# Attention of the first chunk between the q, k and v projections, with the bias table as three tensors, in a hybrid encoder block

## The chip, the cores and the metric

One Trainium2 chip, 8 cores. Each core computes one of the eight batch elements (2048 tokens of 1024 channels) with the same program and all the weights; the cores exchange nothing. The metric is the device time of the slowest core in microseconds (us). The time before the change is a median of three runs.

## The reference

The block computes, for each batch element:

```
x   = LayerNorm_in(x)
u   = x @ W_in              # q 512 | k 128 | v 128 | conv-GLU 1024 | branch gates 2048
y_a = windowed_gqa(q, k, v, rel_bias, sink) @ W_attn_out
y_c = silu(LayerNorm(depthwise_conv31(a * sigmoid(g)))) @ W_conv_out
mix = (sigmoid(g_a) * y_a + sigmoid(g_c) * y_c) @ W_out
h   = LayerNorm1(alpha * x + mix)
out = LayerNorm2(alpha * h + (silu(h @ W_gate) * (h @ W_up)) @ W_down)
```

Attention has 8 query heads in 2 groups that share a key and a value head of 64 channels. A block of 128 queries sees its own block of keys and those on either side, with a relative-position bias by head (masked outside a distance of 128) and a sink logit in the denominator. So 16 query blocks see three key blocks each, the first and the last see two.

## The kernel before

**How the work is tiled.** Tokens go in four chunks (tc) of 512, each of four tiles of 128. `ln_in` (line 531) loads a tile of x, normalises it on VectorE and transposes it into x0T. `glu_block` (560) makes the convolution's input: two projections of 512 tokens, a tanh into `sig` on ScalarE (L566) and a product into `glu` on VectorE (L568). The q, k and v projections are the loop in lines 603 to 627 (L556 with `wqk`, L621 for v), each evicted by ScalarE into qT, kT and vones. The convolution goes through DRAM: glu is stored in four pieces, reloaded transposed as `poly` (634 to 640), and multiplied by tap matrices that VectorE builds (L650) in four groups `conv_mm` (L667, its bias added on VectorE in L671). Its LayerNorm follows: 16 statistics (L481, L484), 16 normalisations (L692), and 16 times four transposes (L701) with a SiLU on ScalarE (L705) into `ycin`.

**Attention** goes in 16 units n, one query block each. `att_front` (717) does, for each of its two or three key blocks, the score products of both groups (L729, one pair on the two halves of the array's rows) into two banks, the scaling and bias on VectorE (L736, one for each bank) and the exp on ScalarE (L742) into one of twelve probability tiles pT. `att_back` (747) does, for each group, the value products (L762), the division on VectorE (L767, L769, L770: add the sink, reciprocal, multiply), and after the second group a transpose (L781) and a copy back into qT (L785). `gate_block` (804) does one eighth of the gated merge of a chunk: two gate projections (L556 with `wga`) with a tanh into `gab` (L813), the products Ya (L822, from attention, needs all four units of the chunk) and Yc (L831, from the convolution), two VectorE steps (L837, L840) and a sum on GpSimd (L843). There are eight gab tiles, so four gate blocks can be open at a time. Then come `mix_tile` (L863) and the feed-forward part (L902, L926).

**What sets the order.** Nothing is ordered by hand. Each operation is added with an engine, an estimated cost and a priority (`sc.prio`, lower is more urgent), and the planner `arrange` (141) simulates the five engines and builds one fixed order for each. On each engine it takes, of the operations that can start at once, the one with the lowest priority value, and otherwise the one that can start first; a switch of ScalarE's table between exp and SiLU is charged with 2.6 us, and a DMA with 2.0 us and then its turn in a single serial stream of 0.19 MB per us. PSUM banks are given out by class (`tr=2, proj=3, sc=4, o=2, y=2, mix=2, gu=6, dn=4, cv=2`). The priorities that matter here: front stage 100 to 135, poly 126, bias loads 140, tap tiles and convolution 155 to 160, its LayerNorm 165, q, k and v of chunk tc at 300 + tc, attention units of chunk c at 400 + 10 c and a little more for each unit, gate blocks of chunk tc at 408 + 10 tc, x0 rows 460.

**What waits for what.** A wait is made for each read and write of the same tensor, and also for bytes that two tensors share: `register` (82) notes the overlaps, and an operation on a tensor waits for all operations, added earlier, on every tensor that overlaps it, whatever part they touch. The byte map is lines 349 to 438. `biast` (399) lies over `lnin` (the two rows of the input LayerNorm, 389) and `sig` (390); the probability tiles pTa and obf (404, 405) lie over the glu weights `wgl` (381); `wao` and `wco` lie over the last wgl and all wqk. SyncE issues the plain loads and stores, GpSimd those that cast to bf16 (the weights).

Of the kernel before, what the change touches and what calls it, by code (L numbers as in the profile page):

```python
# [6 lines left out]
F32 = mybir.dt.float32  # L7
BF16 = mybir.dt.bfloat16
AF = mybir.ActivationFunctionType
ALU = mybir.AluOpType  # L10
# [275 lines left out]
def build():  # L286
    nc = bass.Bass("TRN2", target_bir_lowering=False)

    def din(name, shape):
# [6 lines left out]
    bias_d = din("biasT", [3, 128, 1024])  # L296
# [14 lines left out]
    sc = Sched(dict(tr=2, proj=3, sc=4, o=2, y=2, mix=2, gu=6, dn=4, cv=2),  # L311
               ("xl", "slot", "glu_d", "h_d", "x0_d", "out_d", "gu"))

    def sb(off, shape, dt, name):
        h = nc.alloc_sbuf_tensor_at(name, shape, dt, offset=off)
        nbytes = int(np.prod(shape[1:])) * (4 if dt == F32 else 2)
        assert off >= SBUF_BASE and off + nbytes <= SBUF_TOP, (name, off, nbytes)
        sc.register(name, off, nbytes)
        return h, off + ((nbytes + 31) // 32) * 32

    def sbn(off, n, shape, dt, name):
        hs = []
        for i in range(n):
            h, off = sb(off, shape, dt, "%s%d" % (name, i))
            hs.append(h)
        return hs, off


    o = SBUF_BASE
    ident, o = sb(o, [128, 128], BF16, "ident")  # L330
    ident32, o = sb(o, [128, 128], F32, "ident32")
    small, o = sb(o, [128, C_SMALL], F32, "small")
    hbias, o = sb(o, [128, 16], F32, "hbias")
    esink, o = sb(o, [128, 8], F32, "esink")
    negh, o = sb(o, [128, 8], F32, "negh")
    NST = 8
    stt, o = sbn(o, NST, [128, 12], F32, "st")
    mvX, o = sb(o, [128, 32], F32, "mvX")
    rsX, o = sb(o, [128, 16], F32, "rsX")
    mvC, o = sb(o, [128, 32], F32, "mvC")  # L340
# [9 lines left out]
    YR = R0 + 4 * 8192  # L350
# [15 lines left out]
    def bank(b):  # L366
        return ps[:, b.i * 512:(b.i + 1) * 512]
# [10 lines left out]
    for f in range(8):  # L378
        for w in range(2):
            wga[f + 8 * w] = sb(WG + 2048 * (2 * f + w), [128, 1024], BF16, "wga%d" % (f + 8 * w))[0]  # L380
    wgl, o = sbn(WD_, 8, [128, 1024], BF16, "wgl")
    wqk, o = sbn(o, 6, [128, 1024], BF16, "wqk")
    qT, _ = sb(ER, [128, 4 * S], BF16, "qT")
    kT, _ = sb(KR, [128, S], BF16, "kT")
    vones, _ = sb(KR + 8192, [128, 16 * 130], BF16, "vones")
# [1 line left out]
    lnrow, o = sb(GR, [128, 2 * D], F32, "lnrow")  # L387
    onesr, _ = sb(o, [128, 128], F32, "onesr")
    lnin, o = sb(LS, [128, 2 * D], F32, "lnin")
    sig, _ = sbn(o, 2, [128, 512], F32, "sig")  # L390
    taps, o = sb(TP, [128, 64 * 3 * 16], BF16, "taps")
    cbias, o = sb(o, [128, 512], F32, "cbias")

# [2 lines left out]
    yall, _ = sb(YR, [128, 16 * 512], F32, "yall")  # L396
    tw = [sb(WG + 20480, [128, 16 * 3 * 128], BF16, "tw0")[0], sb(GR, [128, 16 * 3 * 128], BF16, "tw1")[0]]

    biast, _ = sb(LS, [128, 3 * 1024], F32, "biast")
    wao, o = sb(WD_ + 12288, [128, 4 * 1024], BF16, "wao")  # L400
    wco, o = sb(o, [128, 4 * 1024], BF16, "wco")
    assert o <= ER
# [44 lines left out]
    ycv = ycin[:, :].rearrange("p (c r i) -> p c r i", c=4, r=16)  # L447
    qTv = qT[:, :].rearrange("p (h s) -> p h s", h=4)
    vv = vones[:, :].rearrange("p (t g c) -> p t g c", t=16, g=2)
    biasv = biast[:, :].rearrange("p (j c) -> p j c", j=3)  # L450
    woutv = wout[:, :].rearrange("p (k c) -> p k c", k=8)
    waov = wao[:, :].rearrange("p (k c) -> p k c", k=4)
    wcov = wco[:, :].rearrange("p (k c) -> p k c", k=4)
# [14 lines left out]
    def load(kb, dst_ap, src_ap, writes, reads=()):  # L468
        sc.dma("sp", kb, lambda e: e.dma_start(out=dst_ap, in_=src_ap), reads=reads, writes=writes)
# [241 lines left out]

    sc.prio = 140
    for j in range(3):
        load(512, biasv[:, j, :], bias_d[j], [("biast", j)])
    pctr = [0]

    def att_front(n):
        pts = [[], []]
        for j in range(3):
            kb = n + j - 1  # L720
            if not 0 <= kb < 16:
                continue
            Bs = (Bank("sc"), Bank("sc"))

            def f_sc(e, kb=kb, Bs=Bs):
                ins = None
                for g in range(2):
                    r0 = 64 * g
                    ins = e.matmul(bank(Bs[g]).rearrange("p (i q) -> p i q", i=4),  # L729
                                   kT[r0:r0 + 64, kb * 128:(kb + 1) * 128],  # L730
                                   qTv[r0:r0 + 64, :, n * 128:(n + 1) * 128], start=True, stop=True)
                return ins
            sc.add("pe", 0.3, f_sc, reads=[("kT", kb // 4)] + [("qT", i, n) for i in range(4)], writes=list(Bs))
            for g in range(2):
                B = Bs[g]
                sc.add("dve", C_DVE, lambda e, B=B, g=g, j=j: e.scalar_tensor_tensor(  # L736
                    bank(B), bank(B), 0.125, biasv[:, j, g * 512:(g + 1) * 512], ALU.mult, ALU.add),
                    reads=[B, ("biast", j)], writes=[B])
                pi = pctr[0] % NP
                pctr[0] += 1  # L740
                pt = pTb[pi]
                sc.add("act", C_ACT, lambda e, B=B, pt=pt: e.activation(pt[:, :], bank(B), AF.Exp),  # L742
                       reads=[B], writes=[pTn[pi]], table="exp")
                pts[g].append((pi, pt, kb))
        return pts
# [44 lines left out]

    def att_units(us):
        for n in us:
            sc.prio = 400 + (n // 4) * 10 + (n % 4) * 0.2
            for k in range(n, min(n + 2, 16)):
                if k not in fr and k // 4 == n // 4:
                    fr[k] = att_front(k)
            pts = fr.pop(n)
            for g in range(2):
                att_back(n, g, pts[g])
# [310 lines left out]
```

How the kernel before makes its waits and increments, by code:

```python
    def run(self, ename, eng):  # L260
        seen = {}
        def wait(pairs):
            waits = {}
            for sem, val in pairs:
                key = id(sem)
                if key not in waits or waits[key][1] < val:
                    waits[key] = (sem, val)
            for key, (sem, val) in waits.items():
                if seen.get(key, 0) < val:
                    eng.wait_ge(sem, val)
                    seen[key] = val
        for op in self.order[ename]:
            pairs = [d.token for d in op.deps]
            if op.extra is not None:
                pairs.append(op.extra)
            wait(pairs)
            ins = op.fn(eng)
            if op.dma:
                ins.then_inc(op.token[0], 16)
            elif op.sig:
                ins.then_inc(op.token[0], 1)
        wait([o.token for o in self.all if o.dma])
```

## Time and profile before

| | before |
|---|---|
| median of three runs | 916.88 us (915.97 to 917.78) |
| profiled execution, its own time | 915.82 us |
| its span, slowest of 8 cores | 914.3 us (others from 911.4) |
| TensorE busy | 858.4 us, 94% of the span |
| VectorE busy | 504.8 us, 55% |
| ScalarE busy | 244.6 us, 27% |
| GpSimd busy | 198.3 us, 22% |
| DMA moved | 110.62 MB, 121 GB/s in the mean |

How to read it. The profile is one execution, on its slowest core. PE is TensorE's matmul, PEld its weight load (beside PE), DVE VectorE, ACT ScalarE, POOL GpSimd, SP SyncE; a "q" behind a name is the engine's own queue of instructions or DMA issues. L736 is line 736 of the kernel. In a row of instructions "out<-in" names the tensors without buffer numbers, x is the count, and the arrow in brackets says what ended the idle time ahead of it. PEclk is the granted clock of TensorE as a share of its full 2.4 GHz. Times in the trace are in us from the start of the span.

### The profile page before, as it was taken

The page shows a single profiled execution, that of the slowest core. Times are in us where ns is not written, and L with a number is a line of the kernel's source. Part 1 is how long each engine was busy: PE and PEld are TensorE (multiplying, and loading weights), DVE is VectorE, ACT ScalarE, POOL GpSimd, SP SyncE. Part 2 cuts the span into 40 slices and gives each one's busy share as a digit, 9 for nine tenths or more (in the row PEclk, how much of TensorE's full clock was granted, in tenths as well). Part 3 has the DMA queues.
Part 4 walks back from the last instruction along what each step waited for, and adds up shares of the span by engine and source line. Part 5 has one row for each costly group of instructions (what it writes and reads, how often), then busy time and mean ns, then how long its engine had stood idle before and what let it go on. Part 6 is the DMA issues. An engine that isn't in the chain of part 4 may idle for free.

```text
span 914.3 us, 13966 instructions; the slowest of 8 cores (911.4 to 914.3 us)
## 1 busy us (share of the span) xinstructions
PE 858.4 (94%) x4638; PEld 412.8 (45%) x4724; DVE 504.8 (55%) x793; ACT 244.6 (27%) x373; POOL 198.3 (22%) x291
## 2 busy tenths in 40 slices
PE   4899999679999999999999999999999999999994
PEld 1445565534444444444444444444444444444441
DVE  5798348777988967777783212136552121223654
ACT  2233324562635444424332111100001111110000
POOL 4234002214031220523233231112111111100111
PEclk9999999779999999999999999999999999999997
DMA  9876588173342331748779998522345554500321
GB/s 200 197 161 108 124 181 133 55 139 116 117 150 82 116 116 49 182 139 228 172 202 237 167 165 129 83 53 110 116 124 85 84 77 70 82 11 33 107 92 46
DMA packets 47928, 110.62 MB, mean 121 GB/s; under 512 B 12913, under 2 KB 13041, under 8 KB 47473
## 3 DMA queue, kind: packets, MB, share of 16 engines
q0 software_dynamic: 21600, 41.72, 30.3%
q1 hardware_dynamic: 26258, 68.00, 22.5%
q8 instruction: 40, 0.66, 0.3%
q14 instruction: 30, 0.25, 0.1%
HBM read 124.15 MB, written 27.26 MB: 166 GB/s over the span
## 4 chain that ended last, share of the span: by engine, by line
PE 84%; DVE 5%; DMA 4%; issue 4%; ACT 1%; POOL 1%; SPq 0%; DVEq 0%; ACTq 0%; POOLq 0%
PE ps L902 32%; PE ps L556 19%; PE ps L926 17%; PE ps L863 4%; PE ps L831 3%; PE ps L822 2%; DMA h_rows<-xr 2%; PE ps L667 1%; PE ps L729 1%; DMA xr<-x_rows 1%; PE ps L506 1%; DVE st L481 1%; PE ps L701 1%; PE ps L762 1%; DVE ps L736 1%
## 5 line engine op out<-in xcount | busy, mean ns | idle before, releaser
L910 DVE TENSOR_TENSOR hid<-ps,sgb 128x512 bf16<-128x512 f32 x88 | 60.9, 692 | 214.4 <-PE ps L902 211.4
L902 PE MATMUL ps<-hT,wEa 128*128 128x512 bf16 x688 | 153.5, 379 | 1.7 <-DMA xr<-x_rows 0.9
L902 PE MATMUL ps<-hT,wEb 128*128 128x512 bf16 x689 | 153.6, 379 | 0.8
L926 PE MATMUL ps<-wdn,hid 128*128 128x512 bf16 x690 | 151.5, 379 | 0.7
L908 ACT ACTIVATE sgb<-ps 128x512 f32<-128x512 f32 x88 | 52.6, 598 | 313.4 <-PE ps L902 312.6
L556 PE MATMUL ps<-x0T,wga 128*128 128x512 bf16 x492 | 115.9, 379 | 2.3 <-ACT pTb L742 0.7
L926 PEld LDWEIGHTS ps<-wdn,hid 128*128 128x128 bf16 x704 | 68.9, 98 | 83.0
L902 PEld LDWEIGHTS ps<-hT,wEa 128*128 128x128 bf16 x704 | 68.6, 98 | 83.3 <-issue 1.3
L902 PEld LDWEIGHTS ps<-hT,wEb 128*128 128x128 bf16 x704 | 68.7, 98 | 81.9
L843 POOL TENSOR_TENSOR mT<-gab,gab 128x512 bf16<-128x512 f32 x32 | 48.0, 1512 | 131.0 <-DVE gab L837 55.6
L556 PEld LDWEIGHTS ps<-x0T,wga 128*128 128x128 bf16 x512 | 48.7, 98 | 59.8 <-issue 4.5
L813 ACT ACTIVATE gab<-ps,hbias 128x512 f32<-128x512 f32 x64 | 43.8, 688 | 87.9 <-PE ps L556 85.6
L736 DVE SCALAR_TENSOR_TENSOR ps<-ps,biast 128x512 f32<-128x512 f32 x92 | 59.0, 692 | 7.7 <-PE ps L729 7.7
L556 PE MATMUL ps<-x0T,wgl 128*128 128x512 bf16 x251 | 58.2, 391 | 3.0 <-ACT x0T L510 2.5
L863 PE MATMUL ps<-wout,mT 128*128 128x512 bf16 x251 | 57.4, 379 | 0.5 <-DVE rden L769 0.3
L931 DVE SCALAR_TENSOR_TENSOR hr<-hr,ps 128x512 f32<-128x512 f32 x32 | 21.9, 685 | 61.0 <-PE ps L926 61.0
L742 ACT ACTIVATE pTa<-ps 128x512 bf16<-128x512 f32 x71 | 40.8, 599 | 24.7 <-DVE ps L736 23.8
L556 PEld LDWEIGHTS ps<-x0T,wgl 128*128 128x128 bf16 x256 | 25.6, 100 | 34.7 <-issue 6.5
L487 POOL TENSOR_SCALAR rsZ<-mvZ 128x1 f32<-128x1 f32 x16 | 4.7, 291 | 156.2 <-DVE mvZ L484 156.2
L863 PEld LDWEIGHTS ps<-wout,mT 128*128 128x128 bf16 x256 | 24.8, 98 | 29.3 <-issue 0.5
L831 PE MATMUL ps<-ycin,wco 128*128 128x512 bf16 x128 | 33.9, 392 | 4.1 <-ACT ycin L705 2.3
L556 PE MATMUL ps<-x0T,wqk 128*128 128x512 bf16 x152 | 35.3, 379 | 0.4
(96 smaller groups left out, 901.0 us busy)
## 6 DMA issues: line engine op xcount, KB each, us to landing
xa<-x SPq DMA_DIRECT2D x16, 512.0 KB, 6.3
xb<-x SPq DMA_DIRECT2D x16, 512.0 KB, 3.8
x_rows<-xb SPq DMA_DIRECT2D x16, 512.0 KB, 2.8
xr<-x_rows SPq DMA_DIRECT2D x16, 512.0 KB, 5.4
h_rows<-xr SPq DMA_DIRECT2D x16, 512.0 KB, 5.4
hr<-h_rows SPq DMA_DIRECT2D x16, 512.0 KB, 3.3
out<-hr SPq DMA_DIRECT2D x16, 512.0 KB, 2.6
wEa<-wg POOLq DMA_DIRECT2D x22, 256.0 KB, 4.3
```

What stands on the lines that cost most here:

```text
L556: ins = e.matmul(bank(B), w[:, kc, :], x0Tv[tc][:, kc, :], start=(kc == 0), stop=(kc == 7))
L736: sc.add("dve", C_DVE, lambda e, B=B, g=g, j=j: e.scalar_tensor_tensor(bank(B), bank(B), 0.125, biasv[:, j, g * 512:(g + 1) * 512], ALU.mu ...
L742: sc.add("act", C_ACT, lambda e, B=B, pt=pt: e.activation(pt[:, :], bank(B), AF.Exp), reads=[B], writes=[pTn[pi]], table="exp")
L813: sc.add("act", 0.69, lambda e, ga=ga, B=B, w=w: e.activation(ga[:, :], bank(B), AF.Tanh, bias=hbias[:, 8 * w + f:8 * w + f + 1], scale=0. ...
L831: ins = e.matmul(bank(Yc), wcov[:, c, f * 128:(f + 1) * 128], ycv[:, c, :, 32 * tc:32 * tc + 32], start=(c == 0), stop=(c == 3))
L843: sc.add("pool", 1.27, lambda e: e.tensor_tensor(mTv[tc][:, f, :], ga[:, :], gc[:, :], ALU.add), reads=[gan, gcn], writes=["mT%d" % tc] + ...
L863: ins = e.matmul(bank(B), mTv[tc][:, kc, i * 128:(i + 1) * 128], woutv[:, kc, half * 512:(half + 1) * 512], start=(kc == 0), stop=(kc == 7))
L902: ins = e.matmul(bank(B), w[:, kc, :], hTv[tc][:, kc, :], start=(kc == 0), stop=(kc == 7))
L908: sc.add("act", C_ACT, lambda e, G=G, sg=sg: e.activation(sg[:, :], bank(G), AF.Silu), reads=[G], writes=[sn], table="silu")
L910: sc.add("dve", C_DVE, lambda e, U=U, sg=sg, c2=c2: e.tensor_tensor(hid[ffc][:, c2 * 512:(c2 + 1) * 512], bank(U), sg[:, :], ALU.mult), re ...
L926: ins = e.matmul(bank(B), hid[k][:, c0:c0 + 128], wdn[k][:, half * 512:(half + 1) * 512], start=(k == 0), stop=(k == NFF - 1))
L931: sc.add("dve", C_DVE, lambda e, half=half, B=B: e.scalar_tensor_tensor(xs[:, half * 512:(half + 1) * 512], xs[:, half * 512:(half + 1) * ...
```

## The change

The glu weights are laid out in the order c, c+4 instead of 0 to 7 in a row. `sig` moves from behind `lnin` to the start of the yall region (YR). The bias table becomes three tensors, one for each key block, in the same bytes as before. Their loads have priority 122 instead of 140. Units 0 to 3 have priority 301.1 and up instead of 400 and up, all others keep theirs. The paired score products are as they were, and nothing else differs.

```diff
--- before.py
+++ after.py
@@ -378,8 +378,11 @@
     for f in range(8):
         for w in range(2):
             wga[f + 8 * w] = sb(WG + 2048 * (2 * f + w), [128, 1024], BF16, "wga%d" % (f + 8 * w))[0]
-    wgl, o = sbn(WD_, 8, [128, 1024], BF16, "wgl")
-    wqk, o = sbn(o, 6, [128, 1024], BF16, "wqk")
+    wgl = [None] * 8
+    for c in range(4):
+        for w in range(2):
+            wgl[c + 4 * w] = sb(WD_ + 2048 * (2 * c + w), [128, 1024], BF16, "wgl%d" % (c + 4 * w))[0]
+    wqk, o = sbn(WD_ + 16384, 6, [128, 1024], BF16, "wqk")
     qT, _ = sb(ER, [128, 4 * S], BF16, "qT")
     kT, _ = sb(KR, [128, S], BF16, "kT")
     vones, _ = sb(KR + 8192, [128, 16 * 130], BF16, "vones")
@@ -387,7 +390,7 @@
     lnrow, o = sb(GR, [128, 2 * D], F32, "lnrow")
     onesr, _ = sb(o, [128, 128], F32, "onesr")
     lnin, o = sb(LS, [128, 2 * D], F32, "lnin")
-    sig, _ = sbn(o, 2, [128, 512], F32, "sig")
+    sig, _ = sbn(YR, 2, [128, 512], F32, "sig")
     taps, o = sb(TP, [128, 64 * 3 * 16], BF16, "taps")
     cbias, o = sb(o, [128, 512], F32, "cbias")
 
@@ -396,7 +399,7 @@
     yall, _ = sb(YR, [128, 16 * 512], F32, "yall")
     tw = [sb(WG + 20480, [128, 16 * 3 * 128], BF16, "tw0")[0], sb(GR, [128, 16 * 3 * 128], BF16, "tw1")[0]]
 
-    biast, _ = sb(LS, [128, 3 * 1024], F32, "biast")
+    biast, _ = sbn(LS, 3, [128, 1024], F32, "biast")
     wao, o = sb(WD_ + 12288, [128, 4 * 1024], BF16, "wao")
     wco, o = sb(o, [128, 4 * 1024], BF16, "wco")
     assert o <= ER
@@ -447,7 +450,6 @@
     ycv = ycin[:, :].rearrange("p (c r i) -> p c r i", c=4, r=16)
     qTv = qT[:, :].rearrange("p (h s) -> p h s", h=4)
     vv = vones[:, :].rearrange("p (t g c) -> p t g c", t=16, g=2)
-    biasv = biast[:, :].rearrange("p (j c) -> p j c", j=3)
     woutv = wout[:, :].rearrange("p (k c) -> p k c", k=8)
     waov = wao[:, :].rearrange("p (k c) -> p k c", k=4)
     wcov = wco[:, :].rearrange("p (k c) -> p k c", k=4)
@@ -711,7 +713,8 @@
 
     sc.prio = 140
     for j in range(3):
-        load(512, biasv[:, j, :], bias_d[j], [("biast", j)])
+        sc.prio = 122
+        load(512, biast[j][:, :], bias_d[j], ["biast%d" % j])
     pctr = [0]
 
     def att_front(n):
@@ -734,8 +737,8 @@
             for g in range(2):
                 B = Bs[g]
                 sc.add("dve", C_DVE, lambda e, B=B, g=g, j=j: e.scalar_tensor_tensor(
-                    bank(B), bank(B), 0.125, biasv[:, j, g * 512:(g + 1) * 512], ALU.mult, ALU.add),
-                    reads=[B, ("biast", j)], writes=[B])
+                    bank(B), bank(B), 0.125, biast[j][:, g * 512:(g + 1) * 512], ALU.mult, ALU.add),
+                    reads=[B, "biast%d" % j], writes=[B])
                 pi = pctr[0] % NP
                 pctr[0] += 1
                 pt = pTb[pi]
@@ -790,7 +793,7 @@
 
     def att_units(us):
         for n in us:
-            sc.prio = 400 + (n // 4) * 10 + (n % 4) * 0.2
+            sc.prio = (400 + (n // 4) * 10 if n >= 4 else 301.1) + (n % 4) * 0.2
             for k in range(n, min(n + 2, 16)):
                 if k not in fr and k // 4 == n // 4:
                     fr[k] = att_front(k)
```

## Rows read from the trace of the kernel before

**Rows 1.** The page, busy tenths and granted clock in 40 slices of 22.9 us

```profile
PE   4899999679999999999999999999999999999994
...
PEclk9999999779999999999999999999999999999997
```

**Rows 2.** Stretches: length, busy us (count) PE, PEld, DVE, ACT, POOL; clock, DMA, GB/s

```profile
13.00:28.50 15.50, 9.13 (x38) 4.50 (x37) 12.52 (x15) 7.69 (x10) 3.17 (x8) 1.00 1.06 207
114.00:120.50 6.50, 6.45 (x50) 3.67 (x49) 0.02 (x1) 2.35 (x4) 0.00 (x0) 1.00 1.12 231
128.60:135.20 6.60, 6.60 (x45) 3.52 (x44) 0.03 (x1) 2.34 (x4) 1.16 (x2) 1.00 0.37 62
141.00:155.40 14.40, 13.29 (x147) 8.98 (x148) 11.48 (x22) 5.85 (x11) 4.23 (x8) 1.00 0.79 118
155.40:169.70 14.30, 8.52 (x51) 3.75 (x49) 14.12 (x39) 4.75 (x8) 5.40 (x8) 0.91 0.65 141
169.70:183.90 14.20, 11.20 (x68) 10.26 (x68) 7.59 (x18) 12.58 (x18) 1.97 (x4) 0.73 0.00 0
183.90:201.80 17.90, 12.98 (x104) 6.31 (x106) 14.68 (x35) 12.21 (x23) 0.24 (x1) 0.70 0.92 177
201.80:207.00 5.20, 5.17 (x18) 1.90 (x18) 2.97 (x5) 1.48 (x4) 2.39 (x2) 0.72 0.00 0
207.00:351.00 144.00, 140.50 (x882) 64.31 (x899) 118.46 (x197) 69.61 (x116) 33.11 (x23) 1.00 0.31 110
```

**Rows 3.** TensorE's instructions in order of time: start, duration, group

```profile
112.43 1.95 PE L621 MATMUL ps<-wqk,x0T 128*128 128x128 bf16 x32
...
144.51 2.84 PE L667 MATMUL ps<-tw,poly 128*128 128x128 bf16 x48
...
169.69 2.79 PE L701 MATMUL ps<-ident,yall 128*128 128x128 f32 x12 [5.73 <-DVE yall L692]
```

**Rows 4.** ScalarE's instructions in order of time

```profile
171.08 1.28 ACT L705 ACT_TABLE_LOAD   x1 [6.33 <-PE ps L701]
172.37 11.53 ACT L705 ACTIVATE ycin<-ps,small 128x512 bf16<-128x512 f32 x16
...
184.39 1.28 ACT L742 ACT_TABLE_LOAD   x1
```

**Rows 5.** The chain that ended last, in order of time: start, duration, what

```profile
201.83 4.83 PE ps L822 x15
```

**Rows 6.** SyncE's queue in order of time

```profile
114.97 2.10 SPq L469 DMA_DIRECT2D biast<-biasT  x3
```

**Rows 7.** DMA issues: size of one, median us from issue to landing

```profile
biast<-biasT SPq DMA_DIRECT2D x3, 512.0 KB, 8.9
```

**Rows 8.** VectorE's instructions in order of time

```profile
92.85 2.47 DVE L541 SCALAR_TENSOR_TENSOR x0b<-xa,rsX,lnin 128x1024 bf16<-128x1024 f32 x2
...
120.48 2.29 DVE L671 TENSOR_TENSOR yall<-ps,cbias 128x512 f32<-128x512 f32 x3 [6.68 <-PE ps L667]
...
135.23 2.28 DVE L671 TENSOR_TENSOR yall<-ps,cbias 128x512 f32<-128x512 f32 x3 [6.61 <-PE ps L667]
...
141.08 2.49 DVE L736 SCALAR_TENSOR_TENSOR ps<-ps,biast 128x512 f32<-128x512 f32 x4 [0.34 <-PE ps L729]
```

**Rows 9.** Groups by form, 183.9 to 201.83: busy us, mean ns of one

```profile
L736 DVE SCALAR_TENSOR_TENSOR ps<-ps,biast 128x512 f32<-128x512 f32 x16 | 10.3, 690 | 0.0
...
L831 PE MATMUL ps<-ycin,wco 128*128 128x512 bf16 x16 | 5.2, 481 | 2.3 <-ACT ycin L705 2.3
...
L770 DVE TENSOR_TENSOR obf<-ps,rden 128x256 bf16<-128x256 f32 x5 | 2.0, 418 | 0.1
...
L769 DVE RECIPROCAL rden<-rden 128x4 f32<-128x4 f32 x5 | 0.8, 172 | 0.0
L767 DVE TENSOR_TENSOR rden<-ps,esink 128x4 f32<-128x4 f32 x5 | 0.7, 151 | 0.5 <-PE ps L762 0.5
```

**Rows 10.** Groups of VectorE, 98 to 155.4 us

```profile
L736 DVE SCALAR_TENSOR_TENSOR ps<-ps,biast 128x512 f32<-128x512 f32 x9 | 5.9, 693 | 0.4 <-PE ps L729 0.3
```

## The prediction

> **What bounds the kernel now.** First the page: TensorE is busy for almost the whole span, and its granted clock is full, except in two places, slices 8 and 9 of 40 (about 160 to 206 us), where both the busy share and the clock dip [rows 1]. A change to the order of work ahead of the feed-forward part can gain there and hardly anywhere else. Then the table by stretches [rows 2]. From 155.4 to 207 us TensorE is busy for 8.52 + 11.20 + 12.98 + 5.17 = 37.9 of 51.6 us, and weighted with the granted clocks beside them (0.91, 0.73, 0.70, 0.72) that is 7.8 + 8.2 + 9.1 + 3.7 = 28.8 us of work at full clock. So 22.8 us is the ceiling of any gain here. After 207 us TensorE is busy for 140.50 of 144 us at full clock: whatever brings it to that state earlier arrives at the end nearly whole.
>
> Then the chain of waits and the engines, for who holds it in these 51.6 us. (a) 155.4 to 169.7: VectorE, busy 14.12 of 14.30 us, with the 16 statistics of the convolution's LayerNorm and then its normalising; TensorE has used up its filler (eight gate projections fill the eight gab slots) and stands idle for 5.73 us before the first transpose at 169.69 [rows 2, 3]. (b) 169.7 to 183.9: ScalarE, with a table load of 1.28 us and 16 SiLU evictions in 11.53 us, the last ending at 183.9 [rows 4]. (c) 183.9 to 201.8: the rest of the attention of chunk 0. ScalarE switches back [rows 4], and units 1 to 3 run as a chain of score product, VectorE bias, exp, value product and division, until L822, the first product that needs all four units, starts at 201.83 [rows 5]. In these 17.9 us TensorE has 12.98 us of busy time at clock 0.70.
>
> **What the change does, part by part.**
>
> (1) The bias loads. They are now issued at 114.97, behind the stores of glu, because the one table shares its bytes with lnin and with sig; they take 8.9 us to land [rows 6, 7], so no unit can pass its bias step before some 124 us. In the changed kernel sig lies elsewhere, biast2 overlaps nothing of the front stage, and biast0 and biast1 wait only for lnin, whose last reader starts at 92.85 and with its twin takes 2.47 us, so ends at 95.3 [rows 8]. They land at 95.3 + 8.9 = 104 us. Bytes and issues are the same, three of 512 KB: nothing for these two, since SyncE's next issue (the first glu store) waits for glu anyway. biast2 with priority 122 is ready at once, so it goes on SyncE's queue behind the fifth x tile, at 4 to 5 us, ahead of ident32 and cbias (late users). There it meets the x and weight loads, with the DMA share at 1.06 and 207 GB/s [rows 2]. Bounds: 0, because VectorE and not a load paces that stretch (12.52 of 15.50 us busy); at most 0.52 MB / 207 GB/s = 2.5 us if all of it lands on the start. I take 0.5, nearer the busy VectorE.
>
> (2) The weight tiles wgl are put in the order in which the glu blocks use them, so that the probability tiles (written over them) come free block by block. It adds no instruction; its worth is that no exp waits for the last glu block. sig at its new place meets only tiles written much later. Nothing.
>
> (3) The priority. Units 0 to 3 go from 400 to 301.1, that is behind the q, k, v projections of chunks 0 and 1 but ahead of those of chunks 2 and 3 (302, 303). The last they need, v of chunk 1, ends at 114.4 [rows 3]. The units cannot displace the glu blocks, convolution or LayerNorm (100 to 165), which are still ahead of them. VectorE has room just then: it is busy for 0.02 of 6.50 us from 114 and for 0.03 of 6.60 us from 128.6 [rows 2], the idle times of 6.68 and 6.61 us ahead of the convolution's additions [rows 8].
>
> The work to place: chunk 0 has 22 bias steps (four for unit 0, six for each other). Four follow one another in 2.49 us, 0.62 each [rows 8], so 13.7 us; and eight divisions of 0.15 + 0.17 + 0.42 us, overlapped some 0.7 [rows 9], so 5.6. Together 19.3 us of VectorE. Nine bias steps lie ahead of the statistics already [rows 10], which with two divisions is some 7 us. The two idle times add 12.5 us and small ones from 141 to 155.4 (11.48 of 14.40 busy, [rows 2]) 2.9. So 7 + 12.5 + 2.9 = 22.4 us are there for 19.3: all of chunk 0 just fits ahead of the statistics.
>
> (4) What moves with it. The planner (arrange) serves all DMAs one after the other at 0.19 MB per us, so 512 KB are 0.5 / 0.19 = 2.63 us in the plan. The three bias loads are issued behind the stores of glu and ahead of the last reloads of poly [rows 6], and are 7.9 us of plan there. With them gone the last two convolution groups may be planned up to 7.9 us earlier, and the statistics with them. Bounds: 0 (they also need the tap tiles, and their additions share VectorE with attention) and 7.9. The third group starts at 144.51 [rows 3], 9.3 us behind the first addition of the second at 135.23 [rows 8], and its own 2.84 us and the building of tap tiles need part of that: I take the middle, 4. The price is that the idle VectorE time shrinks by the same 4 us, so that 19.3 - 18.4 = 1 us and, since the units wait for one another at the edges, some 4 us in all (two thirds of a unit) is left for after SiLU. The other engines have room. ScalarE is busy for 2.35 + 2.34 + 5.85 = 10.5 of 27.5 us in these three stretches [rows 2], and the exps that move there are fewer than 22, one for each bias step and about as long. On TensorE attention takes at most 9.1 - 3.6 = 5.5 us more there (the full-clock work of 183.9 to 201.8 without the Yc products, 5.2 us at clock 0.70 [rows 2, 9]); its filler comes later by that much and so covers the idle 5.73 us [rows 3]. If it didn't, nothing would be lost, since VectorE holds the chain there. On GpSimd's queue the loads of wco and of the last gate tiles wait for the last projections, and come those 5.5 us later; they are wanted only at the Yc and gate products behind SiLU, so nothing.
>
> **The sum**, against the profiled execution's own time of 915.8 us (span 914.3, and 1.5 around it), 1.1 below the median 916.9. L822 may start when SiLU has ended and the remainder of attention is through. Now 201.8. Then: end of SiLU 183.9, less 4 for the earlier statistics; plus 4 for the remainder; plus 2 for the part of the Yc products (16 in 5.2 us [rows 9]) that the remainder doesn't cover; plus 1 because six bias steps of unit 4 and their products, done by 201.8 now, may then still be to do; plus 0.5 for the start: 183.9 - 4 + 4 + 2 + 1 + 0.5 = 187.4. That is 14.4 us earlier. Nothing is given back behind, with TensorE busy 140.50 of 144 us: 915.8 - 14.4 = 901.4, as a median 902.5. Ends: without earlier statistics and a remainder of 4 the gain is 10; with 7.9 and no remainder it is 22, which is at the ceiling.
>
> What the sum leaves open is the clock. TensorE idles for 5.73 us before 169.69, and the granted clock, 1.00 before, is 0.91 in that stretch and 0.73, 0.70 and 0.72 in the three behind [rows 2, 3], a mixture of its two levels, 2.4 and 1.2 GHz. With the hole filled by attention's 5.5 us it might stay at the upper one; then the Yc products save 0.30 x 5.2 = 1.6 us and the Ya products 0.28 x 4.83 = 1.4 [rows 5, 9], and the median would be 899.5. The sum takes neither. The Trainium skill ("TensorE: Matmul & The Clock Gate", Part 1) says that the array's clock is halved when it idles and freed by sustained work, and the transposes between SiLUs would still leave it partly idle for 11.5 us, so that by the page the low clock stays and with it the 902.5.
>
> **The rivals.**
>
> *Part of the gain (3 to 9 us).* The planner may put fewer units ahead of the statistics, since their products wait for four score banks and twelve probability tiles. From 183.9 to 201.8 there are 16 bias steps [rows 9], so each one more that is left over costs 17.9 / 16 = 1.1 us behind SiLU. Five to ten more give 908 to 913.5. For it: the nine steps ahead of 155.4 now need 14 us from the first at 141.08 [rows 8]. Against: the last convolution groups lay between them.
>
> *Slower.* Every engine runs in a fixed order. If a bias step or division placed between 120 and 155 us waits on the chip for its product or exp, the additions and statistics behind it in VectorE's queue wait too, and the whole chain to SiLU moves. Place: VectorE's queue ahead of 155.4; price: with no overlap each unit's round through four engines costs 4 to 6 us (some three units took 17.9 us behind SiLU, 6 each, at low clock), four units 16 to 24 us, against the 14.4 us of the sum. It decides from 14 us of such waits on; 20 would give 922. Against it: the planner's costs (0.69 for a bias step, against 0.62) are at or above the measured ones, so the plan should hold, and independent projections lie between.
>
> *Table switches.* Now exp and tanh stop before SiLU starts and there is one switch each way, 1.28 us [rows 4]. With units of chunk 1 ready early, exps could be planned in the midst of the SiLUs. By the row a round costs 2.6 us, all in the chain; two rounds 5.2, giving 907.7, within the rival of part of the gain. The Trainium skill ("ScalarE: Activation LUTs", What ACT_TABLE_LOAD costs) adds a drain of 1.38 us to each switch; here the first SiLU starts at 172.37, directly behind the load's end (171.08 + 1.28) [rows 4], so the trace does not show the drain. By the page two rounds would cost 10.7 us.
>
> *Nothing changes.* The bias table may not have been what held the units, and the planner may still place them behind. Their load at 114.97 against a first bias step at 141.08 [rows 6, 8] says that the priority held them too, and that is changed as well; so little is left for this.
>
> *More.* Statistics 8 us earlier and no remainder: 895.
>
> **How the numbers follow.** Forecast (gain 10 to 19) 0.60; part of the gain or table rounds 0.21; more than 19 0.06; no change (within 0.2%, 1.8 us, about what a measurement of this kernel can tell) 0.05; slower 0.08. Faster is 0.60 + 0.21 + 0.06 = 0.87. The range 895 to 913 takes in the forecast's own bounds, the rival of part of the gain but for its worst end and some of the rest, about 0.8.
>
> **What would show it.** Bias loads at about 5 and 95 us on SyncE's queue; the first L736 at 115 to 120 rather than 141; VectorE no longer idle from 114 to 120 and 128 to 135; at least 18 bias steps ahead of the first statistics; statistics starting near 151; one table load each way; L822 starting 12 to 17 us earlier, and the first L902 earlier by the same. Wrong would be: fewer than 13 bias steps ahead of the statistics, TensorE idle between 114 and 155, statistics later than 155.4, or an L822 that is early while the first L902 isn't.

## The result and the profile after

The changed kernel takes 923.59 us (median of five runs, 922.01 to 942.91) against 916.88 before; the ratio is 1.0068 (95% interval 1.0055 to 1.0082). The ratios leave out executions such as that of 942.91, in which two cores had a lower mean granted clock (0.95, the others 0.98), and the medians contain them, so the ratios decide where the two differ. So the changed kernel is slower by 0.7%, where 1.6% faster was forecast, and the time lies outside the range. The profiled execution has a span of 921.1 us on its slowest core, core 6.

The page of the changed kernel, TensorE's busy tenths and granted clock, beside [rows 1]:

```profile
PE   3899998869999799999999999999999999999994
...
PEclk9999999969999899999999999999999999999997
```

Before, the busy share dipped in slices 8 and 9 of 40. Now it is a little low in slices 7 and 8 (138 to 184 us) and lowest in slice 9 (184 to 207 us), and there is a new dip in slice 14 (299 to 322 us).

Its stretches, with the borders and columns of [rows 2]:

```profile
114.00:120.50 6.50, 6.50 (x61) 3.67 (x59) 4.24 (x8) 4.62 (x9) 0.00 (x0) 1.00 1.07 247
128.60:135.20 6.60, 6.60 (x65) 4.17 (x64) 4.74 (x14) 2.98 (x6) 0.00 (x0) 1.00 0.01 2
141.00:155.40 14.40, 12.53 (x127) 8.67 (x128) 12.21 (x30) 3.95 (x7) 3.18 (x6) 0.88 0.76 118
155.40:169.70 14.30, 14.30 (x93) 7.56 (x91) 14.17 (x37) 5.30 (x8) 6.56 (x10) 1.00 0.91 184
169.70:183.90 14.20, 10.48 (x63) 7.41 (x61) 5.29 (x15) 12.56 (x17) 0.00 (x0) 0.88 0.01 1
183.90:201.80 17.90, 10.34 (x80) 5.98 (x81) 13.96 (x30) 15.14 (x25) 0.00 (x0) 0.62 0.00 1
201.80:207.00 5.20, 5.11 (x44) 3.19 (x42) 3.25 (x10) 4.82 (x8) 2.21 (x4) 0.67 0.47 157
207.00:351.00 144.00, 136.56 (x807) 61.99 (x806) 106.30 (x164) 55.77 (x93) 37.06 (x24) 0.98 0.42 127
```

The first half of the forecast is there. The idle time of VectorE from 114 and from 128.6 us is filled (4.24 and 4.74 us busy, 0.02 and 0.03 before), and TensorE is busy for all of the 14.30 us ahead of 169.7, where it had stood for 5.7. VectorE in order of time and SyncE's queue say the same in single rows:

```profile
115.62 3.69 DVE L739 SCALAR_TENSOR_TENSOR ps<-ps,biast 128x512 f32<-128x512 f32 x6 [1.15 <-PE ps L732]
...
152.34 1.28 DVE L483 BATCH_NORM_STATS2 st<-yall 128x6 f32<-128x512 f32 x2
...
164.02 7.39 DVE L694 TENSOR_SCALAR yall<-yall,mvC,rsC 128x512 f32<-128x512 f32 x16
```

```profile
4.53 0.64 SPq L471 DMA_DIRECT2D biast<-biasT  x1
...
96.12 0.81 SPq L471 DMA_DIRECT2D biast<-biasT  x2
```

The first bias steps are at 115.62 instead of 141.08 [rows 8], the loads at 4.53 and 96.12 instead of 114.97 [rows 6], and the first statistics at 152.34 instead of 155.42. By count 18 of the 22 bias steps lie ahead of them, 9 before.

The second half is not there. ScalarE in order of time, against [rows 4]:

```profile
169.82 0.69 ACT L816 ACTIVATE gab<-ps,hbias 128x512 f32<-128x512 f32 x1 [1.04 <-PE ps L558]
170.52 1.28 ACT L707 ACT_TABLE_LOAD   x1
...
179.22 2.12 ACT L707 ACTIVATE ycin<-ps,small 128x512 bf16<-128x512 f32 x3
181.36 1.28 ACT L745 ACT_TABLE_LOAD   x1
182.65 1.57 ACT L745 ACTIVATE pTa<-ps 128x512 bf16<-128x512 f32 x3
...
198.51 1.28 ACT L707 ACT_TABLE_LOAD   x1
199.81 3.45 ACT L707 ACTIVATE ycin<-ps,small 128x512 bf16<-128x512 f32 x5
```

SiLU's table is loaded at 170.52, 0.6 us earlier than before. But after 11 of the 16 SiLUs ScalarE goes back to exp, at 181.36, and works on attention for 17 us. The last five SiLUs run from 199.81 to 203.3, where all 16 were through by 183.9. The products Yc need all of them, the x0 rows need the bytes that the last transposes read, and the first Yc, at 184.04 before, is now at 204.05. TensorE has 10.34 us of busy time at clock 0.62 from 183.9 to 201.8, less than the 12.98 at 0.70 of [rows 2]. Behind 207 us it is busy for 136.56 of 144 us, not 140.50.

Why ScalarE turned back can be read on TensorE:

```profile
151.58 0.39 PE L784 MATMUL ps<-ident,obf 128*128 128x128 bf16 x4
...
157.47 12.25 PE L558 MATMUL ps<-x0T,wga 128*128 128x512 bf16 x56
169.56 0.60 PE L703 MATMUL ps<-ident,yall 128*128 128x128 f32 x4
...
178.50 1.50 PE L703 MATMUL ps<-ident,yall 128*128 128x128 f32 x12 [0.30 <-ACT ycin L707]
179.84 1.89 PE L558 MATMUL ps<-x0T,wga 128*128 128x512 bf16 x8
181.56 1.04 PE L703 MATMUL ps<-ident,yall 128*128 128x128 f32 x8
```

Seven gate projections (56 matmuls, eight for each) run ahead of the first transpose of the LayerNorm. The eighth stands between the transposes of the last SiLUs, from 179.84, and takes some 1.7 us. Before, all eight were over at 164.0, and then TensorE stood idle. A SiLU takes 0.72 us, so ScalarE ran out of them, and there were exps ready: the early attention had left unit 3's behind, and those of chunk 1 followed without a break.

Which transposes held the banks can be read there too. Attention's own transposes (L784) run at 151.58 and then not before 201.61, so at 179.84 both transpose banks were taken by the LayerNorm's. In `arrange` a bank stays taken until the SiLU that reads it has been placed. With two SiLUs not yet placed no transpose may start, so the planner gives TensorE the projection, with 1.74 us by its own costs. ScalarE has two SiLUs of 0.81 us in hand and is free 0.1 us before the next transpose can start. `arrange` places next what can start earliest on any engine, and in this comparison between engines the 2.6 us of the table switch are not counted. They count only in the choice among the operations of one engine that are ready now, and no SiLU is ready until its transposes are placed. So an exp was placed, and the table with it.

### The profile page after: what moved, and what is told of

Same layout as the page of the kernel before. It is cut to its first block, busy times and chain, and to the rows that moved or that the text cites. A ratio compares the mean times of both kernels' runs of the same rounds, so it can differ in the third digit from the quotient of the medians.

```text
span 921.1 us, 14081 instructions; the slowest of 8 cores (916.1 to 921.1 us)
## 1 busy us (share of the span) xinstructions
PE 866.8 (94%) x4724; PEld 415.0 (45%) x4724; DVE 502.9 (55%) x793; ACT 247.1 (27%) x375; POOL 201.4 (22%) x291
## 3 DMA queue, kind: packets, MB, share of 16 engines
q1 hardware_dynamic: 26258, 68.00, 22.2%
## 4 chain that ended last, share of the span: by engine, by line
PE 91%; DVE 3%; ACT 2%; issue 2%; DMA 1%; SPq 0%; POOL 0%; ACTq 0%; DVEq 0%; POOLq 0%
PE ps L905 33%; PE ps L558 22%; PE ps L929 16%; PE ps L866 6%; PE ps L825 3%; PE ps L834 3%; PE ps L508 2%; PE ps L732 1%; PE ps L669 1%; DVE ps L739 1%; DMA lnrow<-lnp 1%; PE ps L765 1%; PE ps L623 1%; PE ps L525 1%; ACT pTa L745 1%
## 5 line engine op out<-in xcount | busy, mean ns | idle before, releaser
L558 PE MATMUL ps<-x0T,wga 128*128 128x512 bf16 x512 | 118.8, 379 | 1.4 <-ACT pTa L745 0.5
L846 POOL TENSOR_TENSOR mT<-gab,gab 128x512 bf16<-128x512 f32 x32 | 50.7, 1590 | 118.1 <-DVE gab L843 62.0
L558 PE MATMUL ps<-x0T,wqk 128*128 128x512 bf16 x160 | 37.6, 383 | 0.0
```

The source lines that it names most:

```text
L558: ins = e.matmul(bank(B), w[:, kc, :], x0Tv[tc][:, kc, :], start=(kc == 0), stop=(kc == 7))
L846: sc.add("pool", 1.27, lambda e: e.tensor_tensor(mTv[tc][:, f, :], ga[:, :], gc[:, :], ALU.add), reads=[gan, gcn], writes=["mT%d" % tc] + ...
```

## The experiments

Marks of all runs, each from the profiled execution (us; first down product is the first of L926):

| kernel | last SiLU ends | first Ya | first down product | median | ratio (95%) |
|---|---|---|---|---|---|
| before | 183.9 | 201.8 | 597.0 | 916.9 | |
| changed | 203.3 | 206.4 | 603.9 | 923.6 | 1.0068 (1.0055 to 1.0082) |
| e1 memory map only | 181.8 | 202.2 | 599.6 | 919.0 | 1.0022 (1.0012 to 1.0032) |
| e3 bias loads at 140 | 203.7 | 206.9 | 604.5 | 922.4 | 1.0059 (1.0042 to 1.0077) |
| e4 priority only | 184.6 | 201.2 | 596.8 | 915.7 | 0.9986 (0.9976 to 0.9997) |
| e5 SiLUs held together | 185.8 | 195.6 | 596.6 | 915.4 | 0.9985 (0.9975 to 0.9996) |
| e6 three transpose banks | 185.3 | 195.5 | 596.8 | 915.0 | 0.9980 (0.9970 to 0.9990) |
| e7 units at 300.1 | 181.8 | 182.8 | 606.8 | 925.2 | 1.0093 (1.0078 to 1.0108) |
| e8 as e5, no x0 steps | 185.4 | 194.8 | 589.5 | 909.0 | 0.9919 (0.9902 to 0.9935) |
| e9 before, no x0 steps | 184.4 | 201.7 | 596.1 | 916.0 | 0.9989 (0.9979 to 0.9998) |
| e10 as e7, small pause | 181.1 | 183.3 | 588.6 | 927.1 | see below |
| e11 as e7, larger pause | 180.0 | 181.0 | 594.8 | 913.9 | 0.9967 (0.9956 to 0.9979) |
| e12 units at 302.1 | 180.0 | 194.2 | 590.4 | 909.8 | 0.9926 (0.9910 to 0.9943) |
| e13 as e5, chunk 2 earlier | 186.3 | 196.1 | 595.7 | 913.8 | 0.9967 (0.9954 to 0.9980) |

**e1, the memory part alone.**

```diff
-        sc.prio = 122
...
-            sc.prio = (400 + (n // 4) * 10 if n >= 4 else 301.1) + (n % 4) * 0.2
+            sc.prio = 400 + (n // 4) * 10 + (n % 4) * 0.2
```

> Only the memory part of the change: wgl interleaved, sig moved, the bias table as three tensors; priorities as before (loads 140, units 0 to 3 at 400). Theory A (the loss of the changed kernel sits in ScalarE's order: five SiLUs are left behind a block of exps, so that the SiLU stage ends at 203 us instead of 184) expects no such split here, one table load each way, and a time within 2 us of the kernel before (916 to 918). Theory B (what costs is the new memory map or the earlier loads, which meet the x and weight loads) expects most of the loss already here, 920 or more.

919.0 us (1.0022), 1 us above the forecast of theory A and well under theory B's. There is one table load each way and no split. The new map costs 2 us on its own, through another plan (six bias steps ahead of the statistics, not nine), and explains at most a third of the loss.

**e3, the bias loads at their old priority.**

```diff
-        sc.prio = 122
```

> The changed kernel with the bias loads back at priority 140. Only SyncE's queue differs from the changed kernel: the loads stand behind ident32 and cbias. Theory A expects the same time as the changed kernel within 1.5 us (922 to 925), with the same five stranded SiLUs. Theory B, in its form that the early load is the cost, expects 917 or less.

922.4 us, with five SiLUs from 200.2 to 203.7. The order of every engine but SyncE is that of the changed kernel. By the medians the early load costs 1.2 us, by the ratios 0.8, and the two intervals overlap, so no difference is shown. It has no visible part in the loss.

**e4, the priority alone on the memory map of before.**

```diff
-            sc.prio = 400 + (n // 4) * 10 + (n % 4) * 0.2
+            sc.prio = (400 + (n // 4) * 10 if n >= 4 else 301.1) + (n % 4) * 0.2
```

> The kernel before with nothing changed but the priority of units 0 to 3, 301.1 instead of 400; the bias table is one tensor and loads at about 115 us as before. Theory A: the split of the SiLUs depends on which exps are ready when a transpose is late, not on the priority as such; here no split is planned, so one table load each way, a first Ya product 2 to 6 us earlier than 201.8, and 911 to 915. Theory C (early attention as such costs: its steps stand ahead of the convolution's additions and delay the LayerNorm chain) expects slower than before, 918 to 923.

915.7 us, no split, 11 bias steps ahead of the statistics. With the bias table only there from about 124 us on, the priority can bring two steps forward and 1.2 us. Theory C falls for so small a move. The gain is smaller than theory A had it: the first Ya is 0.6 us earlier, where it asked for 2 to 6.

**e5, no exp between the SiLUs.** The changed kernel, and in `arrange`:

```diff
+        silus = [op for op in self.all if op.table == "silu" and op.prio < 200]
...
                 for op in ready[e]:
+                    if op.table == "exp" and table == "silu" and any(s.fin is None for s in silus):
+                        continue
```

> The changed kernel with one rule more in the planner: once SiLU's table is loaded, no exp or tanh may be taken before all 16 SiLUs are placed. Theory A: the SiLUs run in one block and end near 187 instead of 203, xb loads near 187, the first Ya near 190, and most of the loss comes back with some of the forecast gain: 908 to 915. Theory C, or any theory in which the split is only a symptom, expects 920 or more. If it comes to 916 to 919, the split explains the loss but the early attention is worth nothing.

915.4 us, 8.2 below the changed kernel by the medians and 7.6 by the ratios. The last rows of ScalarE in that stage:

```profile
182.33 3.46 ACT L710 ACTIVATE ycin<-ps,small 128x512 bf16<-128x512 f32 x5 [0.92 <-PE ps L706]
...
186.28 1.28 ACT L748 ACT_TABLE_LOAD   x1
```

The five SiLUs now run at 182.33, the exps behind them, and the first Ya is at 195.6, 6.2 us earlier than before. But of the 6.2 only 0.4 are left at the first down product (596.6 against 597.0), and the time is 0.15% better than before. Two questions follow: is the cause of the split understood, and where do the 6 us go.

**e6, a third bank for transposes.** The changed kernel without that rule:

```diff
-    sc = Sched(dict(tr=2, proj=3, sc=4, o=2, y=2, mix=2, gu=6, dn=4, cv=2),
+    sc = Sched(dict(tr=3, proj=3, sc=4, o=2, y=2, mix=2, gu=6, dn=4, cv=2),
```

> The changed kernel with three PSUM banks for transposes instead of two (cap tr=3); no rule on the tables. Theory A, in its exact form (the SiLUs split because attention's transposes held a transpose bank, the LayerNorm transposes of one SiLU came late, ScalarE had no SiLU ready and took an exp): with a bank more the 16 SiLUs are in one block without being forced, end at 185 to 187, and the time is that of the kernel with the rule, 914 to 917. If the banks are not the reason, the SiLUs split again and it stays at 921 or more.

915.0 us, the same as with the rule, and the SiLUs are in one block unforced:

```profile
179.84 5.46 ACT L707 ACTIVATE ycin<-ps,small 128x512 bf16<-128x512 f32 x8 [0.20 <-PE ps L703]
...
185.80 1.28 ACT L745 ACT_TABLE_LOAD   x1
```

With the third bank TensorE has transposes to run at that moment, and the eighth gate projection comes behind the last of them. So the lack of a bank is shown to be the cause. The expectation laid the full bank to attention's transposes. That part was wrong: as read above, they were the LayerNorm's own.

**e8 and e9, the x0 rows without their VectorE work.** In e5's kernel and in the kernel before, `x0_rows` leaves out the two steps of `norm`, so the residual input is x and not LayerNorm(x):

```diff
             load(512, xs[:, :], x_d[t * 128:(t + 1) * 128, :], [xn])
-            norm(xs, xn, mvX[:, 2 * t:2 * t + 1], ("mvX", t), rsX[:, t:t + 1], ("rsX", t), lnx, "lnx")
```

> The changed kernel with the rule on the tables, and the two VectorE steps of each x0 row left out (32 steps of 1.2 us, 38 us of VectorE between 190 and 350): the rows are loaded and stored unnormalised, so the residual is x instead of LayerNorm(x). Theory D (VectorE gives back behind 207 us what the front gains, from 6.2 us at the first Ya to 0.4 at the first down product) expects 909 to 912, 4 to 6 us below the kernel with the rule. If the loss behind 207 is only the order of the units, 914 to 916.

> Control for the last one: the kernel before with the same two VectorE steps of each x0 row left out. TensorE is busy for 140.5 of 144 us behind 207 there, so theory D expects hardly a gain, 914 to 917. If it gains as much as the other, VectorE's load costs the same with and without the change and explains nothing of it.

Behind 207 us, e5, then e8, then e9, one row of stretches each:

```profile
207.00:351.00 144.00, 137.22 (x880) 62.11 (x877) 111.64 (x189) 66.58 (x111) 31.22 (x20) 0.99 0.31 103
```

```profile
207.00:351.00 144.00, 139.48 (x915) 64.39 (x913) 82.55 (x178) 67.65 (x113) 25.74 (x22) 1.00 0.34 117
```

```profile
207.00:351.00 144.00, 140.34 (x903) 64.00 (x902) 80.08 (x166) 70.28 (x117) 27.93 (x23) 1.00 0.29 97
```

With the change 32 VectorE steps are worth 6.4 us by the medians (915.4 to 909.0) and 6.1 by the ratios, without it 0.6 (916.6 to 916.0) and 1.0. Of e8's gain 0.8 us is there at the first Ya, since the plan of the front moved too, and 7.1 at the first down product. TensorE's busy time in these 144 us is 137.22 in e5, where VectorE is busy for 111.64, and 139.48 in e8 with 82.55. So what the front gains is given back behind 207 us where VectorE's queue holds attention, gates and rows. In e5's chain of waits an x0 step (L498, 1.04 us at 302.09) stands between the last bias step of unit 11 and that unit's divisions, for which Ya of chunk 2 waits. The order goes with it. Unit 8 ends its bias steps at 279.8 us in e5 and at 264.1 in the kernel before. In e8 it is as late as in e5, 278.3, and in e9 later, 286.1; without the x0 steps the late order costs little.

**e13, the units of chunk 2 earlier.** e5's kernel with

```diff
-            sc.prio = (400 + (n // 4) * 10 if n >= 4 else 301.1) + (n % 4) * 0.2
+            sc.prio = (418.35 if 8 <= n < 12 else 400 + (n // 4) * 10 if n >= 4 else 301.1) + (n % 4) * 0.2
```

> The kernel with the rule on the tables, and chunk 2's units at 418.35 instead of 420, so that unit 8 passes its last bias step near 260 as in the kernel before (264) and in the one with the units at 302.1 (257), and not at 280. Theory G (the front's gain of 6 us is given back because unit 8 comes late and units 8 to 11 then crowd between 280 and 302 ahead of the products Ya of chunk 2) expects TensorE's short stops from 207 to 430 to fall from 7.7 us to about 3, and 910 to 912. If VectorE is the limit there whatever the order of the units, the stops only move, and it stays at 914 to 917.

```profile
207.00:351.00 144.00, 139.95 (x880) 63.45 (x878) 111.23 (x190) 66.33 (x113) 31.23 (x20) 1.00 0.32 108
```

Unit 8 passes its bias steps by 261.5, TensorE gets 139.95 us of the 144, but longer stops come at 366 to 374 us, and TensorE's waits from 207 to 430 us sum to 7.8 us, 8.0 in e5. The time is 913.8, 1.6 us better, neither theory's number. The order of chunk 2 is a part of it, and moving that alone mostly moves the stops.

**e12, the units behind chunk 2's projections.**

```diff
-            sc.prio = (400 + (n // 4) * 10 if n >= 4 else 301.1) + (n % 4) * 0.2
+            sc.prio = (400 + (n // 4) * 10 if n >= 4 else 302.1) + (n % 4) * 0.2
```

> The changed kernel with the units of chunk 0 at 302.1 instead of 301.1, behind chunk 2's projections too: 13 bias steps ahead of the statistics instead of 18, and the SiLUs in one block. Theory A: without the split it must be faster than the changed kernel although fewer steps are early, and with less of the attention early than in the kernel with the rule its first Ya is later: 912 to 917. If early steps are the cost and the split only a part, it lies between the kernel before and the changed one, 918 to 921.

909.8 us, 0.7% faster than before and better than any theory had it, with 13 early bias steps instead of 18. Theory A was wrong on the way there too: it had the first Ya later than in e5, and it is earlier (194.2 against 195.6).

```profile
167.87 1.28 ACT L707 ACT_TABLE_LOAD   x1 [0.91 <-PE ps L703]
169.17 10.81 ACT L707 ACTIVATE ycin<-ps,small 128x512 bf16<-128x512 f32 x16
...
180.47 1.28 ACT L745 ACT_TABLE_LOAD   x1
```

All 16 SiLUs run without a gap in 10.81 us and end at 180.0, 3.9 us earlier than before. With less attention ahead of them all eight gate projections are over at 166.2 here, when the first tiles are normalised (166.3). The first transpose follows at 166.9, and no projection is left to stand between the transposes. The first Ya is 7.6 us earlier, and 6.6 of them are still there at the first down product:

```profile
207.00:351.00 144.00, 141.49 (x920) 64.75 (x918) 115.90 (x204) 70.74 (x117) 29.52 (x20) 1.00 0.32 114
```

VectorE is nearly as busy here (115.90 us) as before (118.46, [rows 2]), so its load alone does not force the giving back. e12's order behind 207 is that of the kernel before, only earlier (unit 8 ends its bias steps at 256.9). Why the plan of the 301.1 kernels falls into the other order was not tried.

**e7, e10 and e11, all of chunk 0 ahead of the statistics.** e7 is the changed kernel with 300.1 in place of 301.1. e10 and e11 also make some gate projections of chunk 0 wait for the last SiLU (f >= 3 in e10, f >= 2 in e11), so that TensorE pauses ahead of the transposes:

```diff
-        sc.add("pe", c_mm(8), f, reads=[wname] + xregs(tc), writes=[B] + list(also))
+        sc.add("pe", c_mm(8), f, reads=[wname] + xregs(tc) + list(more), writes=[B] + list(also))
...
-            proj(wga[f + 8 * w], "wga%d" % (f + 8 * w), tc, B, [("slot", gi)])
+            proj(wga[f + 8 * w], "wga%d" % (f + 8 * w), tc, B, [("slot", gi)],
+                 [("ycin", c) for c in range(4)] if tc == 0 and f >= 3 else [])
```

> The changed kernel with the units of chunk 0 at 300.1 instead of 301.1, so ahead of the rest of chunk 1's projections and of all later ones; all 22 bias steps then lie ahead of the first statistics, and the SiLUs are in one block. Theory A with its remainder (what is left of chunk 0 behind SiLU sets the first Ya product; now nothing is left): first Ya within 5 us of the end of SiLU, so near 188, and 904 to 910. Theory D (the end is set behind 207 us by VectorE, with attention, gates and the x0 rows, whatever the front gains) expects 914 to 916, as with the rule.

> The kernel with the units at 300.1, and the two gate projections of the fourth gate block of chunk 0 made to wait for the last SiLU, so that TensorE has 3 us less filler ahead of the transposes and idles there. In e7_units_first the first Ya came at 182.8, 19 us earlier than before, but TensorE, without an idle stretch from 57 to 182 us, was granted 0.81 from 186 to 349 on all cores. Theory E (the 0.81 follows a long stretch without a pause on all cores; a pause ahead of it prevents it) expects 1.00 or 0.5 there as in all other kernels, and 904 to 910. Theory F (0.81 comes from what runs after 183, gates and attention together at full rate, pause or not) expects it again and 923 to 927.

> The same with the third and fourth gate block held (four projections), about 7 us of TensorE's filler taken away ahead of the transposes, nearly the hole of the kernel before. Theory E: clock 1.00 behind, 909 to 914. Theory F: 0.81 and 925 or more. If the small pause does not help and this one does, the length of the pause matters.

e7 does in the front what the prediction wanted, and more: 22 bias steps ahead of the statistics, and the first Ya right behind the last SiLU.

```profile
182.76 1.46 PE L825 MATMUL ps<-qT,wao 128*128 128x512 bf16 x6
```

That is 19 us earlier than before, and yet the time is 925.2 us. Its stretches behind:

```profile
184.00:202.00 18.00, 18.00 (x73) 7.56 (x71) 12.18 (x14) 4.94 (x9) 9.07 (x5) 0.84 1.04 226
202.00:240.00 38.00, 38.00 (x216) 16.00 (x214) 28.54 (x50) 16.05 (x27) 5.51 (x3) 0.81 0.37 123
240.00:300.00 60.00, 57.34 (x296) 23.47 (x294) 43.66 (x69) 25.21 (x43) 11.85 (x8) 0.81 0.28 97
300.00:351.00 51.00, 50.81 (x269) 21.37 (x268) 34.12 (x58) 18.73 (x32) 10.88 (x8) 0.82 0.24 84
351.00:420.00 69.00, 67.36 (x405) 32.58 (x403) 51.66 (x89) 29.14 (x42) 19.32 (x23) 1.00 0.46 138
```

The granted clock is 0.81 from 186 to 349 us on all eight cores and 1.00 again behind it, with TensorE busy nearly all the time. In all other profiles here only 0.5 and 1.00 occur. 163 us at 0.81 are 31 us less work at full clock; part of it would have been waiting anyhow. The profiled execution of e10 is without it and took 907.07 us. In four of its other five, two or four cores have a mean clock of 0.96, which is the mean of all cores in e7, and spans of 924 to 927 us beside 899 to 904 on the rest. In the fifth all four cores of one die are lower still, at 0.81 to 0.84. So e10's median of 927.1 is of a mixture. In e11 the median is 913.9, and one of eight executions, 931 us, has two cores at 0.96; another, 1018.6 us, has one die at 0.86 to 0.89. No profile caught one of these executions, so that 0.81 was the level in them is inferred from the mean; cores at a lower mean clock occur in single executions of other kernels too.

The expectations set theory E, a long stretch without a pause, against theory F, what runs behind 183 us. For E: e7 is the only profile in which no core's clock is at 0.5 at any time from 15 to 186 us, every core of every other has at least 3.4 us of it there, and the executions with low cores get fewer from e7 to e10 to e11. Against E alone: e5 pauses no longer than e10 does (stops over 0.5 us from 60 to 186 us sum to 4.5 us in both) and has no low core in ten executions. The three kernels that show it all have the units at 300.1 and a first Ya within 2.3 us of the last SiLU, so what runs behind can be a part of it, as in theory F. What sets it off isn't settled: behind 205 us the kernel before runs at 1.00 for 700 us almost without a pause. The Trainium skill ("TensorE: Matmul & The Clock Gate", Seeing it yourself) describes a third state of 13/16, for a whole die, when three or more of its cores run dense products. The value agrees with 0.81; that eight cores run dense products here for most of the span at 1.00 does not.

## Why the prediction was wrong

- **The front, (1) to (3): right.** Loads at 5 and 96 us; a first bias step at 115.6; VectorE's idle stretches filled; 18 bias steps ahead of the statistics (asked for: at least 18); TensorE's 5.7 us filled. The early load was forecast to cost 0.5 us; e3 has 0.8 to 1.2, within the noise.
- **(4), the earlier statistics: right in VectorE, lost on the way.** Forecast 4 us, measured 3.1. The first four tiles are normalised at 165.9, 3.1 us earlier than before (169.0). But the first transpose is at 169.56 (169.69 before), because seven gate projections, now running without a pause, stand ahead of it. With the slower SiLU stage (14.0 us in e5, 11.5 before) SiLU ends at 185.8 even with the split taken away, where the sum had 179.9. I had counted the filler as cover, and not as something that TensorE's fixed order puts in front of the chain.
- **The step that failed: "end of SiLU 183.9, less 4".** It took the SiLU stage as one block that moves. The rival of the table switches was the right one, with the right place, and was priced too low. I wrote 2.6 us for a round, the two table loads. The round cost the block of exps that ran between them, 17 us of ScalarE: the last SiLU ended 19.4 us later than before and 17.5 later than in e5. Of the whole time it cost 8.2 us by e5 and 8.6 by e6 (7.6 and 8.1 by the ratios). I also put it into the part gain and not on the slower side. That it happened hung on little, 0.1 us in the plan.
- **"Nothing is given back behind": wrong.** TensorE's 140.50 of 144 us said that it was the bound in that order. They did not say how much room VectorE had for an order in which TensorE comes earlier. In e5 5.8 of 6.2 us go there, and e8 against e9 shows 6.4 against 0.6 us for the same VectorE steps (6.1 against 1.0 by the ratios). e12 keeps 6.6 of 7.6 us in another order. Why the plan takes the one or the other stays open.
- **The account.** First Ya forecast at 187.4, in e5 at 195.6: 8.2 us short. Given back behind: 5.8. The split: 8.2. Together 22.2, against 923.6 - 902.5 = 21.1 measured.
- **The rival that ended slower** had attention's waits delay VectorE's queue ahead of 155. The statistics came earlier, so that isn't what cost the time. One such wait is there: TensorE stands still for 2.1 us at 140 to 142, where two convolution groups wait for their bank's addition among bias steps. The prediction's own sign of being wrong, TensorE idle between 114 and 155, was met by it.
- **The clock.** It was at 0.88 from 141 to 155.4 us, with that stop, and at 0.62 behind 183.9, where TensorE waited for exps again and again: it followed the idle time. The prediction worked out from the Trainium skill ("TensorE: Matmul & The Clock Gate", Part 1) that it would stay low through the transposes. With the hole filled it was 1.00 from 155.4 to 169.7 and 0.88 from 169.7 to 183.9, against 0.91 and 0.73 before. So that did not come true, and the clock gave no loss of its own there.

## What to carry to other kernels

When an order is planned, a moved piece of work also moves what was filler for it: look which operation the planner can now take at the moment when the critical engine's next operation is late. A table switch costs what is run between the two loads, not the loads; keep a block such as the SiLUs together by a rule, or see that its feeder has a buffer more than it needs. More of the moved work in front is not better by itself: of the kernels that compute the block unchanged, the fastest by its median has 13 early bias steps (e12, 909.8), not 18 or 22. And a busy TensorE shows the bound of the present order only: before a gain in front is counted through to the end, ask which other engine had just kept up.

## What was not expected of the hardware

A granted clock of 0.81 on all eight cores for 163 us in the kernel with the fewest pauses in its front (e7), and by the mean clocks on some cores only in e10, while the denser feed-forward part runs at 1.00. Within executions of e10 the cores with a mean clock of 0.96 end some 23 us behind the others, more than the 19 us that the front had gained at the first Ya.
